# Forget-gate decays of the third attention layer: six rows a head on quarters of the rows, in place of one masked 96-row product

## The reference

```python
log_f = log_sigmoid(f_logit + b_f)                 # (B, S, 16)
cum = cumsum(log_f, axis=1)
s = einsum('bqhd,bkhd->bhqk', q_blk, k) * scale
s = s + c_q[..., :, None] - cum_t[:, :, None, :]   # the decay: cum[q] - cum[k]
s = where(k_pos <= q_pos, s, NEG_INF_2)
p = softmax(s, axis=-1);  o = einsum('bhqk,bkhd->bqhd', p, v)
```

## Time and profile before

| | |
|---|---|
| time, median of 3 runs | 1783.54 us |
| the profiled execution | 1783.37 us, span 1781.6 us |
| granted TensorE clock, mean | 0.998 |
| TensorE busy (matmul) | 1762.7 us, 99% of the span |
| VectorE / ScalarE / GpSimd busy | 992.2 / 811.2 / 727.9 us |
| chain that ended last | PE 89%, DVE 7%, ACT 3% |

### The profile page before, as it was taken

One profiled execution on the slowest core, in us unless ns is written; L12 is line 12 of the kernel. 1 busy time (PEld: TensorE's weight loads), 2 busy tenths in 40 slices (PEclk: granted clock), 3 DMA queues, 4 the chain that ended last, 5 costly groups with the idle time before them and its releaser, 6 DMA issues.

```text
span 1781.6 us, 24874 instructions
## 1 busy us (share of the span) xinstructions
PE 1762.7 (99%) x9776; PEld 1416.7 (80%) x9776; DVE 992.2 (56%) x2091; ACT 811.2 (46%) x1737; POOL 727.9 (41%) x441
## 2 busy tenths in 40 slices
PE   9999999999999999999999999999999999999997
PEld 6787877788888888889776798888877777887676
DVE  4558688564351524254777368755644352567764
ACT  5434455453342323244467345554345343446662
POOL 4534521154686868643322333234332324332122
PEclk9999999999999999999999999999999999999999
DMA  5322320153505151333212232123331322331211
GB/s 173 100 71 72 95 60 25 36 174 93 170 25 177 36 165 48 95 90 93 60 36 83 83 99 72 60 71 94 97 92 50 79 63 90 99 68 38 63 52 72
DMA packets 215032, 147.94 MB, mean 83 GB/s; under 512 B 51825, under 2 KB 197249, under 8 KB 214914
## 3 DMA queue, kind: packets, MB, share of 16 engines
q1 hardware_dynamic: 210592, 137.10, 26.6%
q10 hardware_dynamic: 4322, 9.24, 1.6%
HBM read 144.22 MB, written 2.10 MB: 82 GB/s over the span
## 4 chain that ended last, share of the span: by engine, by line
PE 89%; DVE 7%; ACT 3%; issue 1%; DMA 0%; POOL 0%; SPq 0%; DVEq 0%; ACTq 0%
PE PS L427 24%; PE PS L429 23%; PE PS L428 23%; PE PS L515 6%; PE PS L577 6%; PE PS L601 4%; PE PS L779 1%; DVE PS L1645 1%; ACT X L1172 1%; DVE X L1648 1%; DVE PS L1664 1%; PE PS L1033 1%; PE PS L802 1%; PE PS L1054 0%; DVE P L2188 0%
## 5 line engine op out<-in xcount | busy, mean ns | idle before, releaser
L2291 POOL TENSOR_TENSOR Wl<-Wr,Wh 128x1024 fp32r<-128x1024 f32 (+3 forms) x367 | 601.6, 1660 | 1001.9 <-ACT Wh L1113 1001.6
L427 PE MATMUL PS<-XTl,Wh 128*128 128x512 f32 (+1 forms) x1096 | 412.9, 377 | 1.0 <-DVE KF L1683 0.8
L429 PE MATMUL PS<-XTh,Wh 128*128 128x512 f32 (+1 forms) x1096 | 408.1, 372 | 0.0
L428 PE MATMUL PS<-XTh,Wl 128*128 128x512 f32 (+1 forms) x1096 | 408.0, 372 | 0.0
L1113 ACT CAST Wh<-Wr 128x1024 fp32r<-128x1024 f32 (+5 forms) x274 | 249.3, 931 | 154.5 <-PE PS L429 96.1
L427 PEld LDWEIGHTS PS<-XTl,Wh 128*128 128x128 f32 x1096 | 206.5, 188 | 45.6 <-issue 9.9
L429 PEld LDWEIGHTS PS<-XTh,Wh 128*128 128x128 f32 x1096 | 206.4, 188 | 36.5
L428 PEld LDWEIGHTS PS<-XTh,Wl 128*128 128x128 f32 x1096 | 206.6, 188 | 34.7
L427 PE MATMUL PS<-Wl,XTh 128*128 128x512 f32 (+2 forms) x608 | 227.3, 374 | 1.7 <-DVE XTl L1656 1.2
L429 PE MATMUL PS<-Wh,XTh 128*128 128x512 f32 (+2 forms) x608 | 224.1, 369 | 0.0
L428 PE MATMUL PS<-Wh,XTl 128*128 128x512 f32 (+2 forms) x608 | 224.0, 368 | 0.0
(11 more groups left out here) (342 smaller groups left out, 2748.7 us busy)
## 6 DMA issues: line engine op xcount, KB each, us to landing
Wr<-in_w_in SPq DMA_DIRECT2D x38, 512.0 KB, 3.6
Wr<-in_fox_w_in SPq DMA_DIRECT2D x32, 512.0 KB, 4.2
Wr<-in_w_ffn_gate SPq DMA_DIRECT2D x22, 512.0 KB, 3.9
Wr<-in_w_ffn_up SPq DMA_DIRECT2D x22, 512.0 KB, 3.9
Wr<-in_swa_w_in SPq DMA_DIRECT2D x20, 512.0 KB, 3.8
WP<-in_w_ffn_down SPq DMA_DIRECT2D x9, 1024.0 KB, 9.2
Wr<-in_mla_w_in SPq DMA_DIRECT2D x16, 512.0 KB, 4.1
Wr<-in_mla_w_out SPq DMA_DIRECT2D x16, 512.0 KB, 3.2
```

The costliest lines, as they stand in the source:

```text
L427: pe.matmul(o, l[0], r[1], start=start, stop=False, skip_group_check=again)
L428: pe.matmul(o, l[1], r[0], start=False, stop=False, skip_group_check=again)
L429: return pe.matmul(o, l[0], r[0], start=False, stop=stop, skip_group_check=again)
L2291: ins = raw.tensor_tensor(l[:, cs], r[:, cs], h[:, cs].bitcast(F), sub)
```

## The change

`CB` becomes one tile with both sides, and a second tile `CX` holds for each pair x of heads and each quarter of the rows the six rows of one head side by side. `CX` is filled once, by 24 DMAs that ScalarE issues behind the first queries, when VectorE's last `cb` write is done. Each DMA takes 8 rows of 2 KB and writes one partition of 16 KB. The decays of a pair are then 8 matmuls of 6 rows, on the quarter that `turned_part` would use. `select` and its tiles are gone. TensorE waits with each score for all 24 DMAs (`decay_in`) in place of the pair's `MB`.

```diff
-            CB = [alloc(cm, "CB", [96, T], B16) for _ in range(2)]
-            MB = [alloc(cm, "MB", [96, T], B16) for _ in range(2)]
+            CB, CX = alloc(cm, "CB", [96, 2, T], B16), alloc(cm, "CX", [128, 8, 2, T], B16)
...
+        decay_in = signal("decay_in", 16)
...
+            def decay_part(x):
+                def operands(u, i, n):
+                    r = 64 * (i in (0, 2)) + 32 * u
+                    return CX[r:r + 6, x, 0, tile(i)], CX[r:r + 6, x, 1, 0:n]
+
+                return operands
+
...
-                                  (lambda u, i, n: (CB[0][:, tile(i)], MB[u][:, 0:n]), paired)],
-                           [by_act.at(s, f"q{x}"), by_dve.at(s, f"k{x}"), by_dve.at(s, "mb", x, 1)])
+                                  (decay_part(x), paired)],
+                           [by_act.at(s, f"q{x}"), by_dve.at(s, f"k{x}"), decay_in.at("all")])
...
             queries(s, "q0", 0)
+            e.wait_ge(by_dve.at(s, "cb"))
+            for r in range(6):
+                for g in range(4):
+                    act.dma_start(CX[32 * g + r:32 * g + r + 1, :, :, :], CB[16 * r + g % 2:16 * r + 16:2, :, :]).then_inc(*decay_in.next("all"))
             for kind, x in fox_steps:
...
                 for j in range(2):
-                    ve.tensor_scalar(CB[j][32 * k:32 * k + 32, :], FP[:, :], CST[0:32, C_FOX + 2 * j:C_FOX + 2 * j + 1],
-                                     CST[0:32, C_FOX + 2 * j + 1:C_FOX + 2 * j + 2], mult, add).then_inc(*by_dve.next())
+                    ve.tensor_scalar(CB[32 * k:32 * k + 32, j, :], FP[:, :], CST[0:32, C_FOX + 2 * j:C_FOX + 2 * j + 1],
+                                     CST[0:32, C_FOX + 2 * j + 1:C_FOX + 2 * j + 2], mult, add).then_inc(*by_dve.next(s, "cb"))
...
-            def select(x):
-
-                if x:
-                    e.wait_ge(scores_full.at(s, x - 1, 1, 3))
-                e.wait_ge(by_dve.now())
-                for u in range(2):
-                    h = 2 * x + u
-                    ve.tensor_scalar(MB[u][:, :], CB[1][:, :], CST[0:96, C_SEL + h:C_SEL + h + 1], None, mult).then_inc(*by_dve.next(s, "mb", x, u))
...
-            select(0)
             fox_job("v0")
...
                     maxima(s, x, sm)
-                    if x < 7:
-                        select(x + 1)
```

More of the change, by code:

```diff
@@ L343, in program @@
         norm_in = [signal(f"norm_in{j}", 16) for j in range(2)]
+        decay_in = signal("decay_in", 16)
         row_zero, row_in = signal("row_zero"), signal("row_in", 16)
         stored = [signal(f"stored{i}", 16) for i in range(NT)]
-        signals = [row_zero, row_in, cst_in, *x_loaded, *x_again, *gain_in, *raw_in, *pair_in, weight_hi, weight_lo, weight_used, psum_full, scores_full,
+        signals = [decay_in, row_zero, row_in, cst_in, *x_loaded, *x_again, *gain_in, *raw_in, *pair_in, weight_hi, weight_lo, weight_used, psum_full, scores_full,
                    turned_full, values_full, by_act, by_dve, by_pool, *gla_in, *cmp_in, mask_in, sink_in, bias_in, *norm_in, *stored]
```

## The result

The changed kernel took 1794.91 us (median of 4 runs, 1792.97 to 1795.84), the kernel before 1783.82 us beside it (4 runs, 1783.27 to 1784.19): a ratio of 1.0062, 95% interval 1.0049 to 1.0075. It is slower, by 11.1 us where 5.5 were forecast, and 0.6 us outside the range.

A forecast was written before the change was run, and what follows sets the result against it. TensorE was taken to bound the kernel, busy 236.00 of 236.00 us in fox attention. Stop +8.6, clock +2.0, decays -5.1 gave +5.5 on 1783.37: 1788.9, plus 0.17 for the median, 1789.0 us; range 1783.8 to 1794.3.

The forecast's parts named there:

- part 3: ScalarE's wait and 24 DMA issues (0.47 us each, 11.3 us) ahead of rounding v0.3, delaying TensorE; clock loss added.
- over 0.6 each: Sign in the changed trace: the forecast is wrong if ScalarE's DMA issues take over 0.6 us each.
- The stop: TensorE stands in front of v0.3, from 1272.97 to 1281.6: +8.6 us, bounds 0 and 19.
- cb: VectorE's chain before the copies: last cb ready at 1266.4, between 1266 and 1275, with GpSimd mostly idle.
- R3: Rival on VectorE's chain: cb not earlier, at 1275.04; stop 17.2 us, sum +14.1, total 1797.6 us; chance 0.06.
- The clock: TensorE's clock drops in the stop; about 4 us of work then run at half: +2.0 us, between 0 and 2.8.
- R2: Rival: shorter stop, from issues of 0.40 us or a clock staying up; 1785.2 to 1787.0 us; chance 0.16.
- The quarters: Part 1, fox decays on TensorE's quarters: 2 x 0.50 + 6 x 0.69 = 5.1 us saved, between 4.2 and 6.0.
- the saving should arrive in full: Fox values on TensorE: copies of turned probabilities still end 1.8 us ahead, so the 5.1 us saved is kept.
- R4: Rival on the decays: six rows do not lie side by side, nothing saved; +10.6 us, 1794.1 us; chance 0.06.
- The signals written one after another: Decay matmuls' six completion signals, some 26 ns each: 0.16 us a pair, an estimated 1.3 us off the saving.
- `select`: Part 2, VectorE: removing 16 instructions, 5.5 us beside a never idle TensorE, saves 0; bound 0 to -0.2 us.

The follow-up runs named there:

- rounding first: The changed kernel with ScalarE rounding v0.3, q1, k1 and q2 ahead of its wait for cb; 1795.61 us, ratio 1.0070.
- TensorE kept busy: The changed kernel with 57 matmuls, their result unused, in front of v0.3's wait; 1792.12 us, ratio 1.0053.
- version by pairs: The changed kernel with v0.3 rounded first, 4 copy DMAs per pair of heads, and TensorE waiting only before the second product; 1778.64 us, ratio 0.9971.
- two queues: The changed kernel with 12 of the 24 DMAs issued by SyncE beside ScalarE's 12; 1786.57 us, ratio 1.0021.

## Why the prediction was wrong

**The step that failed** is one term of part 3: "24 x 0.47 = 11.3 us". It was 24 x 0.66 = 15.9 us, beyond the bound of 13.2. The seven issues in the earlier trace rows all read from HBM; these read from SBUF, which no row of before showed and which costs 0.2 us or more an issue. That alone is 4.6 us of the stop. The prediction had named the gap ("in no row") and then put the bounds at 0.40, from like things, and 0.55, from no row at all; the unlike thing lay outside both. Its own sign of being wrong, "over 0.6 each", is the one that came.

**The stop**, forecast 8.6, measured 13.3: 4.6 from the issues and 0.45 from the scan, which I had let shrink by 0.5 us, less 0.3 because the way from the last issue to TensorE took 3.6 us and not 3.9. The scan takes 2.65 us as in the earlier trace rows, though GpSimd is idle for its last 1.1 us: nothing was to be had there. The mechanism, the wait and the path were as forecast; a term of the sum was too small.

**cb** at 1266.85 for 1266.4: the reading of the earlier trace rows together, that the work held up was what slowed the chain, was right. R3 is out, and rounding first shows the other side of it: with GpSimd at work again, cb is as late as before.

**The clock**: +2.0 forecast, 2.3 in the profile, 2.1 against TensorE kept busy. It fell later than the earlier trace rows suggested, not before 4 us of standing in place of 2.4, which did not matter for a stop this long. R2 is out.

**The quarters**: 2 x 0.57 + 6 x 0.76 = 5.7 us by the rows, 0.6 more than counted, since the stage has only 0.1 us over its columns (0.43 - 0.32); but "the saving should arrive in full" was wrong by 0.7. In the turn that follows score 7, TensorE, now ahead, meets banks that ScalarE's exponentials have yet to free:

```profile
1477.38 2.73 PE L515 MATMUL PS<-CST,P 128*128 128x128 f32 x20
1480.22 0.47 PE L427 MATMUL PS<-XTl,Wh 128*128 128x512 f32 x1
```

2.84 us to the next weights; the same turn took 2.16 in the timeline of PE before:

```profile
1465.60 2.40 PE L515 MATMUL PS<-CST,P 128*128 128x128 f32 x20
1467.76 0.48 PE L427 MATMUL PS<-XTl,Wh 128*128 128x512 f32 x1
```

TensorE pauses twice in the later turn, and both pauses end just behind an exponential of ScalarE's (its signals stand at 1479.42 and 1480.08). Net 5.0, near the 5.1 of the sum and the 5.2 us of the version by pairs; that the net is so near the sum is luck, 0.6 us more saved and 0.7 given back. R4 is out, though its 1794.1 lies near the measured time: the decays did become short, and the stop was longer. The signals written one after another, which the Trainium skill ("TensorE: Matmul & The Clock Gate", section "The cost: per-tile semaphore tail") would put at an estimated 0.16 us a pair, take nothing from TensorE: 768 columns are 0.32 us and the whole stage is 0.43, of which the change of shape behind it costs 0.1 in the earlier trace rows too. The trace does have them one after another: two decays whose ends stand 3 ns apart signal 34 ns apart (1298.565 and 1298.599). But TensorE's next stage starts at 1298.70, ahead of the last of them at 1298.82, so the saving loses nothing to them. Here the measurement decides.

**`select`** was worth nothing, as forecast: VectorE is 14.6 us less busy (977.6 for 992.2), and no stretch of TensorE's is shorter for it.

**Not foreseen**: 1.8 us ahead of the layer in this execution, the start and the stretch in swa.

**Two small slips** in the prediction's figures change little: issues of 0.40 alone give +3.8 and not +3.5 in R2 (1787.3 us), and its own three upper terms add up to 1792.6, not 1792.8.

In the sum: the layer costs 10.6 us in the profile where 5.5 were forecast, and 4.7 of these 5.1 are the stop; clock and saving are within half a microsecond of their terms. The remaining 0.5 of the 11.1 is no more than what lies ahead of the layer.

## What to carry to other kernels

Where an in-order engine feeds a pipeline (here ScalarE's rounding of weights), whatever is put into its stream costs its issue time times its count to everything behind it, and the slack of the feed, not the engine's busy share, says how much is free. Cut a preparation so that the first consumer's share comes first and has its own semaphore: 8 issues in place of 24, with the rest spread behind later work, turned 11 us lost into 5 won. And a price for an operation whose source or destination no row shows needs wider bounds than the rows of its relatives.

## What the runs showed of the hardware that I had not expected

An issue of a DMA that reads SBUF holds ScalarE for 0.62 to 0.76 us in a row, one that reads HBM for 0.28 to 0.47; it depends on the rows on both (from SBUF 7 rows 0.76, 6 rows 0.72, 8 rows to one partition 0.66, 16 rows 0.62). SyncE pays about the same (9.08 us for 12, beside ScalarE's). How long TensorE's granted clock of 2.4 GHz holds while it stands varies: 2.4 us at the end of the program before, 3 us with two queues (0.50 from 1276, the last matmul ended at 1272.8), over 4 us in the changed kernel, 5 us with rounding first (1.00 from 1280 to 1283 and 0.50 from 1284, the last matmul ended at 1278.0). Matmuls of 6 rows lie side by side on quarters just as those of 32 rows do.
